# A two-block transformer kernel on one core: where five weight splits stand around the first index scores

## The reference, cut to what matters

```python
h = rms_norm(x, attn_norm[l])
proj = h @ w_in[l]
(aq, ak, av, iq, ik, iw, bq, bf, bi, bg, ...) = jnp.split(proj, split_pts, axis=-1)
...
logits = jnp.einsum('bthd,bsd->bths', iqb, ik32)          # 8 index heads of 64
score = jnp.einsum('bths,bth->bts', jax.nn.relu(logits), iwb) * idx_scale
...
_, sel = lax.top_k(score, topk)
```

## Time and profile before

| | before |
|---|---|
| time, median of 3 runs | 1477.79 us (1475.24 to 1487.32) |
| the profiled execution's own time | 1480.03 us |
| its span on the core | 1478.3 us |
| PE busy | 1392.3 us, 94% |
| DVE busy | 964.0 us, 65% |
| ACT busy | 534.9 us, 36% |
| mean granted TensorE clock | 0.975 of full |

### The profile page before, as it was taken

One profiled execution on the slowest core, in us unless ns is written; L12 is line 12 of the kernel. 1 busy time (PEld: TensorE's weight loads), 2 busy tenths in 40 slices (PEclk: granted clock), 3 DMA queues, 4 the chain that ended last, 5 costly groups with the idle time before them and its releaser, 6 DMA issues.

```text
span 1478.3 us, 18974 instructions
## 1 busy us (share of the span) xinstructions
PE 1392.3 (94%) x7110; PEld 1085.5 (73%) x7110; DVE 964.0 (65%) x1638; ACT 534.9 (36%) x882; POOL 53.4 (4%) x45
## 2 busy tenths in 40 slices
PE   6889999999997798999999999999999999988889
PEld 5659898866765466888788788888769854566677
DVE  6438678877667656764646755543499667668773
ACT  6348444433225633243323422432223221124421
POOL 0000000000004500000000000000000020000000
PEclk9899999999998899999999999999899999989999
DMA  6203211232121213543334334232422213520001
GB/s 249 72 29 115 72 43 58 78 95 102 66 77 51 72 51 138 189 149 108 115 145 168 143 143 157 74 118 79 144 62 82 84 57 98 187 86 1 1 1 57
DMA packets 40891, 141.05 MB, mean 95 GB/s; under 512 B 13280, under 2 KB 17632, under 8 KB 28768
## 3 DMA queue, kind: packets, MB, share of 16 engines
q1 hardware_dynamic: 35616, 131.05, 25.4%
q10 hardware_dynamic: 5184, 8.78, 1.6%
HBM read 128.94 MB, written 8.39 MB: 93 GB/s over the span
## 4 chain that ended last, share of the span: by engine, by line
PE 76%; DVE 15%; ACT 3%; DMA 3%; issue 2%; DVEq 0%; ACTq 0%; SPq 0%
PE turn L734 21%; PE score L734 17%; PE score L719 9%; PE sum L734 9%; PE sum L719 5%; DVE ring_r L1964 3%; DMA ring<-wstream 3%; PE turn L963 2%; PE score L1198 2%; PE score L872 2%; PE sum L1316 2%; ACT heads_r L1424 1%; DVE rows L1970 1%; PE turn L856 1%; PE sum L894 1%
## 5 line engine op out<-in xcount | busy, mean ns | idle before, releaser
L1964 DVE TENSOR_TENSOR ring_r<-ring,heads_r 128x1024 fp32r<-128x1024 f32 (+2 forms) x161 | 186.4, 1158 | 190.9 <-ACT heads_r L1424 187.7
L1424 ACT ACTIVATE heads_r<-ring 128x1024 fp32r<-128x1024 f32 (+2 forms) x161 | 161.9, 1005 | 139.7 <-PE turn L734 70.3
L734 PE MATMUL score<-h_sb_r,heads_r 128*128 128x512 f32 x368 | 147.3, 400 | 0.0
L734 PE MATMUL turn<-tiles_r,heads_r 128*128 128x512 f32 x368 | 143.2, 389 | 0.0
L734 PE MATMUL turn<-h_sb_r,heads_r 128*128 128x512 f32 x336 | 131.0, 390 | 1.0 <-DVE work L1970 1.0
L734 PE MATMUL score<-x_sb_r,heads_r 128*128 128x512 f32 x224 | 95.9, 428 | 1.8 <-DVE ring_r L1964 1.8
L734 PE MATMUL score<-x_sb_r,ring_r 128*128 128x512 f32 x224 | 90.8, 405 | 0.0
L734 PEld LDWEIGHTS score<-h_sb_r,heads_r 128*128 128x128 f32 x368 | 71.2, 193 | 12.8 <-DVE tiles_r L1964 0.2
L734 PEld LDWEIGHTS turn<-tiles_r,heads_r 128*128 128x128 f32 x368 | 69.1, 188 | 14.1
L734 PEld LDWEIGHTS turn<-h_sb_r,heads_r 128*128 128x128 f32 x336 | 63.1, 188 | 15.3 <-DVE work L1970 1.4
L734 PE MATMUL turn<-wide_r,heads_r 128*128 128x512 f32 x188 | 73.1, 389 | 0.0
(11 more groups left out here) (459 smaller groups left out, 3115.2 us busy)
## 6 DMA issues: line engine op xcount, KB each, us to landing
ring<-wstream SPq DMA_DIRECT2D x91, 1024.0 KB, 4.9
ring<-wstream SPq DMA_DIRECT2D x16, 704.0 KB, 4.5
ring<-gated SPq DMA_DIRECT2D x6, 1024.0 KB, 6.5
gated<-tiles ACTq DMA_DIRECT2D x18, 256.0 KB, 2.0
ring<-wstream SPq DMA_DIRECT2D x4, 840.0 KB, 4.6
x_sb<-xT SPq DMA_DIRECT2D x4, 512.0 KB, 7.9
x_sb<-xT ACTq DMA_DIRECT2D x1, 2048.0 KB, 8.2
ring<-wstream SPq DMA_DIRECT2D x3, 512.0 KB, 3.7
```

What stands on the lines that cost most here:

```text
L734: return pe.matmul(out, a, w, **k) if moving else pe.matmul(out, w, a, **k)
L1424: step(act.activation(head_piece(p), chunk(name)[:, c:c + cols], ACT.Identity), f"head {p}")
L1964: step(dve.tensor_tensor(out, a, b, op), name)
```

## The change

Nothing is computed otherwise, and no instruction is added or taken away; five rests, three heads and nothing else change their place.

- VectorE: rests 6 and 7 are made ahead of the wait for `have av` and the scaling of the index weights, rest 8 behind it; rests 9, 10 and 11 are made behind `index added` 1, 2 and 3.
- ScalarE: head 8 stays behind the drain of ik 0; heads 9, 10 and 11 are made behind the index relus 1, 2 and 3, where before they stood ahead of relu 0.

```diff
@@ ScalarE
+            next(units)
+            weight_heads()
             for _ in units:
-                weight_heads()
-            weight_heads(2)
+                pass
             units = project(PROJ1B)
             for i in range(24):
...
                      f"index relu {i}", score_done)
+                if i in (1, 2, 3):
+                    weight_heads()
                 if i in (8, 14, 20):
                     next(units)
                     weight_heads()
@@ VectorE
             rms_scale("attn", lambda k: sm("g_attn")[:, k:k + 1], X_HEAD, before=lambda: weight_rests(2))
+            weight_rests(2)
             dve.wait_ge(gemm_done, at("have av"))
             tt(ROW[:, :, 128:136], ROW[:, :, 128:136], ROOT.unsqueeze(2).broadcast_to([P, NT, 8]), ALU.mult)
-            weight_rests(6)
+            weight_rests()
...
-                if i in (9, 15, 21):
+                if i in (1, 2, 3, 9, 15, 21):
                     weight_rests()
```

## The result

| | before | changed |
|---|---|---|
| median | 1481.12 us (8 runs, 1475.24 to 1487.32) | 1468.32 us (8 runs, 1466.83 to 1473.87) |
| ratio | | 0.9928, 95% interval 0.9908 to 0.9949 |
| the profiled execution, its span | 1480.03, 1478.3 us | 1467.87, 1466.1 us |

The account below looks back on a forecast made before the run. TensorE, busy 94% of the span, was taken as the bound, losing time only to waits or lower clock. 2.2 + 1.5 + 3.3 + 0.5 + 2.5 = 10.0 us took the median from 1477.8 to 1467.8 us, range 1462 to 1475.

Parts of the forecast that it names:

- The first wait: TensorE idle ahead of ik 0 until a VectorE rest ends; making rests 6 and 7 earlier gains 2.2 us.
- The second wait: TensorE idle 3.79 us ahead of index 2; relu 0 no longer behind heads 9 to 11 gains 3.3, leaving 0.5 us.
- The clock behind them: Full clock kept after both waits: 1.5 us in ik 0, 0.5 in index 2, 2.5 in the half of bf 1.
- The reason that I gave for the clock: Highest value, 4.5 us, taken: both slow stretches begin exactly as idle ends; pauses of 0.52 and 0.63 us have none behind.
- The moved work costs nothing: Moved heads and rests on ScalarE and VectorE stay hidden, adding 0 us; 1.8 us to spare at relu 2.
- Nothing takes it back later: From index 5 on, order and spacing are as before; pause-free TensorE from 120 to 160 us keeps the whole gain.
- rival 3: Given back later: a later stage's wait ends at a fixed time, giving up to 1477.8 us; chance 0.05.
- Rival 1: Waits go but slow stretches come elsewhere in the stage; only 5.5 us gained, so 1472.3 us; chance 0.13.
- rival 2: New wait for a late relu or addition in the index stage; only 6.7 us stay, 1471.1 us; chance 0.07.
- rival 4: More than the sum: half the clock loss from 460 to 520 us goes too, giving 1462.8 us; chance 0.08.
- rival 5: Slower: clock falls at the index stage's first pause and stays low, 4 us per third, up to 1500 us; chance 0.03.
- The range and the time: Whole kernel: median 1467.8 us, 0.68% less, within 1462 to 1475 us.

Follow-up runs that it names:

- first part: Kernel before with only rests 6 and 7 moved ahead of the wait for the drained rows and the index-weight scaling; ratio to before 0.9975.
- filled gaps: Kernel before with 9 unread matmuls added ahead of ik 0 and 16 ahead of index 2, both waits kept; ratio to before 0.9978.
- three heads in a row: Changed kernel with heads 9 to 11 all behind relu 1 and their rests behind addition 1; ratio to before 0.9952.
- run by twos: Changed kernel with a half tile after every second index score instead of every third, drains and heads moved along; ratio to before 0.9961.

## Why the prediction was right

- **The first wait (2.2 us).** Right, and slightly too small; A fell by 2.4 us in every kernel that has the first part (by 3.3 where the drain was moved as well). The listed idle is not the whole delay: a row matmul is listed with 0.27 us, but the next one starts 0.11 us behind it, so a wait behind it costs 0.16 us more than its idle, 2.23 + 0.16 = 2.39. In the same way the 0.63 us wait ahead of the last row block cost 0.87 us of A. Rest 6 ran at 44.49, ahead of the need by 3 us as computed.
- **The second wait (3.3 us) and its 0.5 us remainder.** Right: 0.53 us of idle are left ahead of index 2.
- **The clock behind them (1.5, 0.5 and 2.5 us).** Right for the trace that was read, and the filled gaps show the cause for the second wait. As a term for the median it was too large, and taking its highest value was the weak step: traced again, the kernel before lost 1.7 us in B and 1.6 in C, and B lost 0.1 us in two other executions with the 2.2 us idle. The means are 0.8 us over the four executions with the first idle, and 2.5 us over the three traces with the second (3.0, 3.0 and 1.6). With these the sum is, as an estimate from few traces, 2.4 + 0.8 + 3.3 + 2.5 = 9.0 us; the two comparisons measured 10.7 us (7.5 to 13.6) and 8.9 us (6.1 to 11.7).
- **The reason that I gave for the clock** failed in one half: that slow stretches begin exactly at the end of an idle time. In the kernel before, traced again, they began 1.4 and 1.2 us later (at 52.4 and 69.3), and with one head ahead of relu 0 index 2 was still fast behind the idle time. The shorter pauses of 0.52 to 0.73 us, eight in each trace of the changed kernel, had none behind them.
- **The moved work costs nothing.** Right; I allowed 1.8 us at relu 2, and three heads in a row made it 2.2 us late without a loss.
- **Nothing takes it back later.** Right for this change, since PE's order and with it the cover of the ranking stayed the same. The run by twos shows how near a neighbour of rival 3 lies: there a wait of 7.3 us for the ranking took back more than the stage had gained. The ranking is not fixed in time, though, as rival 3 has it; it moves with the end of the index scores.
- **Rival 1 (the clock is not given back)** did not come: 1.00 from 50 to 80 us. Its remark that something besides the idle time has a part was right nevertheless.
- **Rivals 2, 4 and 5** did not come either. For rival 2, no wait for a relu is longer than 0.73 us. For rival 4, the clock of the later stage was 0.80 instead of 0.77, and of the 12.2 us by which the span fell only 0.7 lie behind the recurrence's start. For rival 5, the clock was at 1.00 all through the index stage.
- **The range and the time.** The time came within 0.5 us of the forecast, while the median of the kernel before was 3.3 us higher in this comparison than in its first three runs, so that the medians differ by 12.8 us and not by 10.0. Part of the closeness is luck: by the estimate above the sum was about 1 us too large for the mean.

## What to carry to other kernels

Look at what a waiting engine could have done already: two rests that needed nothing of the awaited row block stood behind the wait for it, and three heads that nobody needed yet stood ahead of the relu for which TensorE waited. The price of such a wait is its idle time and the lower clock that may follow, and the clock's part has to be read from more than one execution. Before work is put into the pauses of a chain, see what starts at the chain's end: by twos the pauses went, but the ranking behind them came later and its wait cost more than they had.

## What the runs showed of the hardware

- The clock's cost was not in proportion to the idle time: 0 behind 0.5 to 0.7 us of idle; 1.6 us behind 1.62 and 2.71 us (one trace each); 0 or 1.5 to 1.6 us behind 2.2 us (two executions each); 1.6 us (once) or 3.0 us (twice) behind 3.79 us; and 2.1 and 2.6 us behind 7.3 us, less than the most behind 3.79. In the first of the last two the granted clock was 0.59 already from 122 to 124 us, while PE still waited, so part of the slow time cost nothing. The Trainium skill (TensorE: Matmul & The Clock Gate, Part 1) says that the number of slow matmuls at the start of a kernel varies from run to run of one kernel. The traces agree for the start (the first 6 to 14 matmuls are slow in the 14 traces), and they show a like variation behind an idle time in mid-kernel (C of 12.28 and 10.88 us in one program).
- The start differs by as much between executions of the same instructions: the row blocks began at 36.83 us (6 slow matmuls at the start) to 38.49 us (14 of them) over 14 traces in which nothing ahead of them was changed. A difference of 1.7 us between two single traces says nothing about a change, which is why D is counted from there.
